# Dilated attention of one block: dense scores against all keys, or two sparse parts over a residue order

## The reference, cut to what matters

```python
DILATED_PATTERNS = ((128, 1), (512, 4), (2048, 16))
def dilated_window_attention(q, k, v, rel_bias, dilation, half_steps):
    """Each query attends to positions i + j*dilation, |j| <= half_steps.
    Returns normalised output (B,H,S,dh) f32 and log-sum-exp (B,H,S) f32."""
    ...
def mixer_dilated(q, k, v, rel_bias):
    outs, lses = [], []
    for window, dilation in DILATED_PATTERNS:
        o, lse = dilated_window_attention(q, k, v, rel_bias, dilation, window // (2 * dilation))
        ...
    w = jax.nn.softmax(jnp.stack(lses, 0), axis=0)
    return jnp.einsum('pbhs,pbhsd->bhsd', w, jnp.stack(outs, 0))
```

## Time and profile before

| what | value |
|---|---|
| median of three executions | 4218.14 us |
| the profiled execution, by the same clock | 4229.26 us |
| its span | 4227.5 us |
| PE, DVE, ACT, POOL busy, share of the span | 90%, 50%, 47%, 29% |
| attention stage, dilated heads (first to last unit) | 187.4 us of the span |
| attention stage, latent heads (first to last unit) | 218.0 us of the span |

### The profile page before, as it was taken

One profiled execution on the slowest core, in us unless ns is written; L12 is line 12 of the kernel. 1 busy time (PEld: TensorE's weight loads), 2 busy tenths in 40 slices (PEclk: granted clock), 3 DMA queues, 4 the chain that ended last, 5 costly groups with the idle time before them and its releaser, 6 DMA issues. The chain is left out here.

```text
span 4227.5 us, 55120 instructions
## 1 busy us (share of the span) xinstructions
PE 3820.9 (90%) x20567; PEld 3209.4 (76%) x20567; DVE 2119.5 (50%) x3777; ACT 1981.5 (47%) x3487; POOL 1233.9 (29%) x732
## 2 busy tenths in 40 slices
PE   8989997969986999999488875797999999999998
PEld 6879996847755777887388875797888768888886
DVE  3348875267754333320566757674234237533453
ACT  5248766337756545522366654564324234323331
POOL 0024430000004322311133244121631103876541
PEclk9999998969998999999699997998999999999999
DMA  3744223479957222222322212113653112222542
GB/s 118 251 134 118 51 51 105 184 273 420 421 241 255 90 80 80 89 94 74 90 61 79 80 55 79 46 46 115 227 161 117 68 50 90 87 88 85 188 148 98
DMA packets 336536, 548.38 MB, mean 130 GB/s; under 512 B 116451, under 2 KB 209507, under 8 KB 325219
## 3 DMA queue, kind: packets, MB, share of 16 engines
q1 hardware_dynamic: 318348, 478.76, 34.1%
q10 hardware_dynamic: 10720, 39.85, 2.4%
q0 software_dynamic: 7200, 26.22, 1.6%
HBM read 400.63 MB, written 144.11 MB: 129 GB/s over the span
## 5 line engine op out<-in xcount | busy, mean ns | idle before, releaser
L2739 POOL TENSOR_TENSOR mid_w_lo<-mid_w_raw,mid_w_hi 128x1024 fp32r<-128x1024 f32 (+1 forms) x64 | 153.0, 2395 | 406.2 <-ACT mid_w_hi L2927 406.2
L3473 POOL TENSOR_TENSOR end_w_lo<-end_w_raw,end_w_hi 128x1024 fp32r<-128x1024 f32 x60 | 147.2, 2460 | 334.4 <-ACT end_w_hi L3815 334.3
L3097 PE MATMUL mid_ps<-mid_w_hi,mid_xT_hi 128*128 128x512 f32 x576 | 229.0, 398 | 2.7 <-DVE mid_xT_lo L2801 2.7
L3097 PE MATMUL mid_ps<-mid_w_lo,mid_xT_hi 128*128 128x512 f32 x576 | 224.7, 390 | 0.0
L3097 PE MATMUL mid_ps<-mid_w_hi,mid_xT_lo 128*128 128x512 f32 x576 | 224.7, 390 | 0.0
L4131 PE MATMUL end_ps<-end_w_hi,end_xT_hi 128*128 128x512 f32 x544 | 214.7, 395 | 0.0
L4131 PE MATMUL end_ps<-end_w_hi,end_xT_lo 128*128 128x512 f32 x544 | 212.3, 390 | 0.0
L4131 PE MATMUL end_ps<-end_w_lo,end_xT_hi 128*128 128x512 f32 x544 | 211.9, 390 | 0.0
L957 DVE SCALAR_TENSOR_TENSOR moe_w_lo<-moe_wgu,moe_gcol,moe_w_hi 128x512 fp32r<-128x512 f32 x272 | 185.5, 746 | 7.7 <-ACT moe_w_hi L1097 7.7
L343 ACT ACTIVATE att_pT_hi<-att_pT_ps 128x512 fp32r<-128x512 f32 x256 | 139.1, 596 | 99.7 <-PE att_pT_ps L36 99.6
L1097 ACT ACTIVATE moe_w_hi<-moe_wgu,moe_gcol 128x512 fp32r<-128x512 f32 x272 | 173.2, 715 | 2.5 <-DMA moe_wgu<-in_w_gate_up 2.5
(11 more groups left out here) (641 smaller groups left out, 11565.8 us busy)
## 6 DMA issues: line engine op xcount, KB each, us to landing
moe_wgu<-in_w_gate_up SPq DMA_DIRECT2D x34, 2048.0 KB, 11.6
moe_wd<-in_w_down SPq DMA_DIRECT2D x34, 1024.0 KB, 14.1
mid_w_raw<-in_w_in SPq DMA_DIRECT2D x60, 512.0 KB, 4.0
end_w_raw<-in_w_ffn_out SPq DMA_DIRECT2D x44, 512.0 KB, 3.7
end_w_raw<-in_w_ffn_in SPq DMA_DIRECT2D x40, 512.0 KB, 4.3
expert_rows<-moe_out ACTq DMA_DIRECT2D x34, 512.0 KB, 11.3
in_tail<-mid_y SPq DMA_DIRECT2D x56, 256.0 KB, 2.1
qkvT<-mid_conv SPq DMA_DIRECT2D x24, 512.0 KB, 4.4
```

The source lines that it names most:

```text
L2739: pool.tensor_tensor(w_lo[:, c % 2, 2 * q:2 * q + 2, 0:wid], w_raw[:, 2 * q:2 * q + 2, 0:wid], w_hi[:, c % 2, 2 * q:2 * q + 2, 0:wid].bitc ...
L3097: ins = pe.matmul(o_, lhsT, rhs, start=(k == 0 and part == 0), stop=(k == KC - 1 and part == 2))
L3473: pool.tensor_tensor(halves(w_lo, piece), w_raw[:, 2 * q:2 * q + 2], halves(w_hi, piece).bitcast(F32), ALU.subtract).then_inc(w_split, 1)
```

## The change

The tokens are put in residue order when x is loaded: first all tokens that are 0 modulo 4, then 1, 2 and 3; outputs are stored back in token order, in four transfers each. A new function `attend_both` replaces `attend_heads` for this stage (the second layer keeps `attend_heads`). It alternates one dilated head (four units) and one latent head (eight units), so a pair of heads has 12 units and the stage 96.

A dilated unit covers 256 queries with four segments of 256 scores: two "near" segments (128 queries of all four classes against 64 keys of each class, from reordered queries `q_near`) and two "far" segments (128 queries of one class against the 256 keys of this class). Each segment has its own maximum, exponential, sum and product with values; for the product the turned weights are the stationary operand, sixteen matmuls of 128 columns. ScalarE copies the low half of each outcome out of PSUM and VectorE adds the high half into `keep`. When a dilated head's four units are through, its near outcomes with their maxima and sums (66 floats a row) are stored to DRAM and loaded again in the order of the far ones (`move_near`); VectorE and ScalarE find the weights of the two parts (`highest`, `share`), and GpSimd merges them (`merge`). Latent units are computed as before. The bias rows shrink from 2048 to 1184 floats a head (three banks), and a dilated head's table comes in ten transfers, its values in seven.

```diff
+STRIDE = 4
+NEAR, AFAR = 96, 512
+BIAS = (2 * STRIDE - 1) * NEAR + AFAR
...
+def attend_both(nc, name, ident_dram, dilated, latent):
+    SPARSE_UNITS, SEGS, SEG = 4, 4, 2 * P
+    jobs = [job for pair in zip(dilated, latent) for job in pair]
...
+                def load_table(j):
...
+                    for w in range(2):
+                        sp.dma_start(view[:, w + 1, 0], first).then_inc(table_in[i % 2], 16)
+                        sp.dma_start(view[:, w, 1], second).then_inc(table_in[i % 2], 16)
+                    sp.dma_start(view[:, 0, 0, :, EDGE:], first[:, :, EDGE:]).then_inc(table_in[i % 2], 16)
+                    sp.dma_start(view[:, 2, 1, :, 0:EDGE], second[:, :, 0:EDGE]).then_inc(table_in[i % 2], 16)
+                    for c in range(STRIDE):
+                        sp.dma_start(table[c * BLOCK:(c + 1) * BLOCK, i % 2, 3 * SEG:], far[c]).then_inc(table_in[i % 2], 16)
...
+                def move_near(j):
+                    i = rank[j]
+                    sp.wait_ge(kept, sparse_by[last_unit[j]])
+                    for c in range(STRIDE):
+                        dst = jobs[j]["near"][c * CLASS:(c + 1) * CLASS].rearrange("(t u) d -> u t d", u=BLOCK)
+                        sp.dma_start(dst, keep[c * BLOCK:(c + 1) * BLOCK, i % 2, 0]).then_inc(near_out, 16)
+                    sp.wait_ge(near_out, 16 * STRIDE * (i + 1))
+                    sp.dma_start(keep[:, i % 2, 2], jobs[j]["near"].rearrange("(t p) d -> p t d", p=P)).then_inc(near_in, 16)
+
+                def store(j):
+                    if sparse[j]:
+                        sp.wait_ge(merged, rank[j] + 1)
+                    else:
+                        sp.wait_ge(o_out, rank[j] + 1)
+                    for c in range(STRIDE):
+                        src = o[:, j % 2, c * NT // STRIDE:(c + 1) * NT // STRIDE]
+                        sp.dma_start(jobs[j]["out"][c], src).then_inc(o_stored[j % 2], 16)
+
+                for i in range(H // 2 + 1):
+                    if i < H // 2:
+                        load(2 * i)
+                        load(2 * i + 1)
+                    if i:
+                        move_near(2 * i - 2)
+                        store(2 * i - 2)
+                        store(2 * i - 1)
...
+                def weigh_sparse(n):
...
+                    for g in range(SEGS):
+                        i = 2 * t + g % 2
+                        for b in range(2):
+                            v = near_both[:, rank[j] % 2, i + b] if g < 2 else v_both[:, j % 2, 2 * t + b]
+                            for k, part in enumerate((pT_hi, pT_lo)):
+                                ins = pe.matmul(oT_ps[:, g * P:(g + 1) * P], split_at(part, n)[:, 2 * g + b], v,
+                                                start=(b == 0 and k == 0), stop=(b == 1 and k == 1))
...
+                    if n >= 5 and is_sparse[n - 5]:
+                        act.wait_ge(weighed, weighed_by[n - 5])
+                        act.activation(low[:, n % 2], oT_ps[:].rearrange("p (g d) -> p g d", d=P)[:, :, DV:], ACT.Copy).then_inc(low_set, 1)
...
+                    for g in range(SEGS):
...
+                        ch.add(dve.tensor_tensor_reduce(biased[:, n % 2, here], s_ps[:, n % 2, here], table[:, i, at:at + SEG],
+                                                        1.0, -3e38, ALU.add, ALU.max, keep[:, i, g // 2, w, DV:DV + 1]))
...
+                def highest(j):
+                    both = keep[:, rank[j] % 2, 1:3]
+                    dve.wait_ge(near_in, 16 * (rank[j] + 1))
...
+                for n in range(U + 6):
+                    for j in range(0, H, 2):
+                        if n == last_unit[j] + 7:
+                            highest(j)
+                    if n >= 5 and n - 5 < U and is_sparse[n - 5]:
...
+                        dve.wait_ge(low_set, sparse_by[n - 5])
+                        dve.tensor_tensor(keep[:, rank[j] % 2, 0:2, 2 * t:2 * t + 2, 0:DV], found, lows, ALU.add).then_inc(kept, 1)
...
+                        if not sparse[j] and n == last_unit[j] + 6:
...
+                            dve.tensor_tensor(o[:, j % 2], o_ps[:], inverse[:, i % 2].unsqueeze(2).to_broadcast([P, NT, DV]), ALU.mult).then_inc(o_out, 1)
...
+                for j in range(H):
+                    if j:
+                        split_queries(j)
+                    if sparse[j]:
+                        order_queries(j)
+                    if j:
+                        split_keys(j)
+                    split_values(j)
...
+                    if sparse[j] and j:
+                        merge(j - 2)
...
-                for b in range(4):
-                    pe.matmul(ps[0:A_HEADS, 4 + b], values[:], onehot[:, b * BANK:(b + 1) * BANK], start=True, stop=True).then_inc(hot_done, 1)
+                for b in range(BIAS_BANKS):
+                    wid = min(BANK, BIAS - b * BANK)
+                    pe.matmul(ps[0:A_HEADS, 4 + b, 0:wid], values[:], onehot[:, b * BANK:b * BANK + wid], start=True, stop=True).then_inc(hot_done, 1)
...
-    attend_heads(nc, "att", ident, dilated + latent)
+    attend_both(nc, "att", ident, dilated, latent)
```

More of the change, by code:

```diff
@@ new lines, in bias_constants, with reach @@
+def bias_constants(T, buckets, max_distance, patterns):
+    block, edge = P // STRIDE, P // STRIDE // 2
+    steps = np.arange(NEAR)[None] - (block + edge - 1)
+    near = (STRIDE * steps + np.arange(1 - STRIDE, STRIDE)[:, None]).reshape(-1)
+    far = STRIDE * (np.arange(AFAR) - (T // STRIDE - 1))
+    def reach(rel, pairs):
+        n = np.abs(rel)
+        return sum(((n % d == 0) & (n // d <= w // (2 * d)) & (n < T)).astype(np.float64) for w, d in pairs)
+    assert all(d == 1 or d % STRIDE == 0 for w, d in patterns)
+    rel = np.concatenate([near, far])
+    count = np.concatenate([reach(near, [(w, d) for w, d in patterns if d == 1]), reach(far, [(w, d) for w, d in patterns if d > 1])])
@@ L467, in dilation_constants, with by_class @@
     onehot = (np.arange(buckets)[:, None] == bucket[None]).astype(np.float32)
-    count = sum(((n % d == 0) & (n // d <= w // (2 * d)) & (n < T)).astype(np.float64) for w, d in patterns)
     log_count = np.where(count > 0, np.log(np.maximum(count, 1)), -1e30)
     return np.concatenate([onehot, log_count[None].astype(np.float32)], 0)
+def by_class(rows):
+    return np.ascontiguousarray(rows.reshape(-1, STRIDE, rows.shape[1]).transpose(1, 0, 2).reshape(rows.shape))
 def rotary_tables(T, theta, half):
@@ L2155, in table_step @@
                         sp.wait_ge(rows_in, 16 * (h + 1))
-                        sp.dma_start(skew[h].rearrange("(p w) -> p w", w=W), raw[:, 0:W]).then_inc(rows_out, 16)
+                        for c in range(STRIDE):
+                            rows = P // STRIDE
+                            at = c * (rows * BIAS + NEAR - rows)
+                            dst = skew[h, at:at + rows * BIAS].rearrange("(p w) -> p w", w=BIAS)
+                            sp.dma_start(dst, raw[c * rows:(c + 1) * rows, 0:BIAS]).then_inc(rows_out, 16)
                     else:
@@ L4210, in table @@
-    def table(h):
-        return skew[h:h + 1, P - 1:P - 1 + P * W - P].rearrange("h (p w) -> (h p) w", w=W - 1)[:, 0:W - P]
-    dilated = [dict(depth=A_DIM, dv=A_DIM, q=qkT_a[h * A_DIM:(h + 1) * A_DIM], k=qkT_a[AW + h * A_DIM:AW + (h + 1) * A_DIM],
-                    v=tiles(v_a[:, h * A_DIM:(h + 1) * A_DIM]), out=tiles(mixed[:, h * A_DIM:(h + 1) * A_DIM]),
-                    scale=A_DIM ** -0.5, bias=table(h)) for h in range(A_HEADS)]
-    latent = [dict(depth=NOPE + ROPE, dv=B_DIM, q=qkT_b[h], k=qkT_b[B_HEADS + h],
-                   v=tiles(v_b[:, h * B_DIM:(h + 1) * B_DIM]),
-                   out=tiles(mixed[:, AW + h * B_DIM:AW + (h + 1) * B_DIM]), scale=(NOPE + ROPE) ** -0.5, bias=None) for h in range(B_HEADS)]
@@ L4219, in build_program, with tables, block, far @@
-    attend_heads(nc, "att", ident, dilated + latent)
+    mixed, near = dram("mixed", (T, AW + B_HEADS * B_DIM)), dram("near", (A_HEADS, T, A_DIM + 2))
+    def tables(h):
+        rows, width, pitch = P // STRIDE, BIAS - 1, STRIDE * NEAR
+        def block(ahead):
+            at = (STRIDE - 1) * NEAR + rows - 1 + ahead
+            flat = skew[h, at:at + P * width].rearrange("(p w) -> p w", w=width)
+            return flat[:, 0:pitch].rearrange("p (c z) -> p c z", z=NEAR)[:, :, 0:rows]
+        def far(c):
+            at = c * (rows * width + NEAR - rows) + (2 * STRIDE - 1) * NEAR + P - 1
+            return skew[h, at:at + rows * width].rearrange("(p w) -> p w", w=width)[:, 0:3 * P]
+        return block(0), block(rows), [far(c) for c in range(STRIDE)]
@@ new lines, in by_class_out @@
+    def by_class_out(columns):
+        return mixed[:, columns].rearrange("(h p c) d -> c p h d", c=STRIDE, p=P)
+    dilated = [dict(depth=A_DIM, dv=A_DIM, q=qkT_a[h * A_DIM:(h + 1) * A_DIM], k=qkT_a[AW + h * A_DIM:AW + (h + 1) * A_DIM],
```

(4 more changed lines are left out.)

446 lines of the change are left out of this document (428 added, 18 removed).

## The result

The changed kernel took 4265.69 us (median of four executions, 4254.07 to 4266.53), the kernel before 4219.65 us beside it: ratio 1.0101, 95% interval 1.0082 to 1.012. It is 46 us slower; the forecast was 4220.5 us, with 4180 to 4256 as its range. The profiled execution took 4265.32 us, its span is 4263.2 us, 35.7 us more than the profiled span of before.

The account below looks back on a forecast made before the run. PE's own issue was taken to bound the stage before the change. Stage +1.9, later start +2.2, last store +1.3 and front -3.0 sum to +2.4 us on 4218.1: 4220.5 us, range 4180 to 4256.

Parts of the forecast that it names:

- The circle: SP's list and VectorE's wait for the near part feed each other: A + B = 53.5 us a pair, six pairs.
- A: From the normalising through SP's loads and the near part's trip to its landing: 23.3 us, bounds 18.0 and 27.
- first pair: Start of the stage up to the first normalising, with no move behind loads: 63.5 us.
- last pair: Six steps remaining behind the last circle: 22.8 us.
- B: VectorE's steps from the near part's arrival to the next normalising: 30.2 us, ends 27 and 31.5.
- the three latent loads: Latent queries, keys and values ahead of the near stores: issued from 12.7 us, 4.2 us of transfers, ending about 18.1.
- rival 4: SP's queue stalls in issuing the small table and value pieces, A = 27: +22 us, 4242.5 us, chance 0.17.
- The fall of the clock: PE stands about 6 us in VectorE's wait, then one step runs at the lower clock: 1.7 us added in B.
- rivals 2 and 3: Sparse weighing: 2, bound by moving columns, 0.06 us, 4208.5 us, chance 0.05; 3, float32 price, 0.222 us, 4245 us, chance 0.12.
- rival 1: The near part's move is nearly hidden: A = 18.0, B = 28.0, 46.0 us a pair, 4175.5 us, chance 0.14.
- The front: Before the stage, the one-hot product shrinks from 2048 to 1184 columns: -3.0 us, bounds -3.0 and 0.
- The tail: The stage's last store becomes four issues: 1.3 us more.

Follow-up runs that it names:

- e7_start: Changed kernel with the first latent head's queries and keys loaded before the first table and values, and split before the first queries are ordered: span 4263.6 us.
- best2: Changed kernel with merge three units later, latent loads behind the near part's trip, first latent head early: 4197.57 us, ratio 0.9933 to the kernel before.
- e1_no_trip: Changed kernel without the near part's four stores, load and VectorE's wait for them (merge takes rows that don't belong together): span 4193.2 us.

## Why the prediction missed, step by step

The circle held as a mechanism. One of its halves, A, was sized too short, and a wait of the first pair was put at nothing. The stage came out 29.8 us longer than forecast (449.1 us where 417.3 + 1.9 was forecast), and by the parts of the sum: six circles 21.2, first pair 10.8, last pair -2.2. (The sum began at 275.60 us; counted from the first score at 273.45 its first pair is 63.5 + 2.2 = 65.7 us.)

**The trip, A (27.3 for 23.3): the step that failed most.** Four terms, means over the circles. First near store 16.7 us after the normalising's end against 14.3: the table's pieces took 6.8 us, not 5.0, as one or two of the short-run pieces held the queue for 1.3 to 2.2 us, and the values 3.8, not 3.3. The four near stores 2.5 us to issue, not 1.5. From there to the load 4.5, as forecast (4.3). Landing 2.9, not 3.2. Another 0.7 is the normalising itself: A begins at its start in the table, at its end in the prediction, which counts it in B. By the prediction's bounds A is 26.6 for 23.3 and B 30.5 for 30.2. One step of the sum had no row: the three latent loads, issued from 12.7 us on with 4.2 us of transfers, end by these figures at 16.9 and not at 18.1; the 4.5 us measured from the last near store to the load leave the end as it was. I took the middle, "since the unloaded issues are the commoner rows"; but a list whose engines are 0.86 busy is not unloaded, and the upper bound, 27, was nearly the value. That was rival 4, with 4242.5 us; the rest of the miss lies elsewhere. I had held eight small stores without a stall against it, which ran with the DMA engines 0.24 busy (2148.7 to 2152.7 us). The Trainium skill's price for small transfers ("DMA: Bandwidth & Descriptors", section "Bandwidth", measured there on transfers that GpSimd issues) would, by an estimate, have made that rival's surplus about twice as large; A at 27.3 does not agree with that.

**The first pair (76.5 us from the first score to the first normalising, forecast 65.7).** I gave it no wait. But GpSimd's list has the first values ahead, for which it waits 3.4 us, and then splits the latent queries and keys one after another; PE waited 5.0 us for the keys. Its clock had fallen to the lower level at about 281 us, ahead of that wait, when PE had stood 2.2 us for VectorE, and came back only at 301 us. GpSimd's split of the keys, and PE's last transposes ahead of the wait and first latent score, in order of time:

```profile
285.33 2.34 POOL L926 TENSOR_TENSOR att_k_lo<-att_kT,att_k_hi 96x1024 fp32r<-96x1024 f32 x1
```

```profile
280.81 1.94 PE L40 MATMUL att_pT_ps<-att_ident,att_p 128*128 128x128 f32 x8 [2.16 <-DVE att_pT_lo L878]
287.77 0.76 PE L677 MATMUL att_s<-att_k_hi,att_q_hi 96*128 96x512 f32 x1 [5.02 <-issue]
```

e7_start and best2 took 6.1 and 12.8 us off the first normalising by changing that order; from the first score to it they take 66.1 and 64.6 us, with the clock at its upper level from 277.9 and 273.8 us on, so without this wait the forecast's 65.7 holds. The prediction read GpSimd's passes for the later pairs and not for the first.

**B (29.8 for 30.2): right in sum, in part by luck.** The fall of the clock was forecast at 1.7 us; an early and a late return differ by about 1 us, and no run isolates what the fall costs in whole. The units themselves were dearer than forecast, which e1_no_trip shows without any wait: its pairs took 45.6 us against 43.3, of which 1.9 in the four sparse steps (3.15, 4.36, 4.37 and 3.20 us, means over the circles, for 4 x 3.3) and 0.4 in the first latent one. In each of the first three of these VectorE's `neg_top` stands behind a GpSimd pass (0.4 to 0.6, 0.6 and 1.7 us in place of 0.17). I had priced it by an estimate of 0.1 us. How much of the 1.9 us these operations make up, no run isolates.

**What held.** Weighing matmuls of 128 columns start 0.11 us apart, the row that I chose over both bounds, so rivals 2 and 3 fall; the 81 ns of the Trainium skill ("TensorE: Matmul & The Clock Gate", "Back-to-back issue gap") do not agree with this float32r stream. PE in order of time:

```profile
310.04 0.28 PE L711 MATMUL att_oT_ps<-att_v_both,att_pT_lo 128*128 128x128 f32 x1
310.15 0.27 PE L711 MATMUL att_oT_ps<-att_v_both,att_pT_hi 128*128 128x128 f32 x1
310.26 0.28 PE L711 MATMUL att_oT_ps<-att_v_both,att_pT_lo 128*128 128x128 f32 x1
```

Latent steps with sparse weighing take 4.1 us (the first, with its fold, 4.9), those without 3.2 to 3.6, free sparse steps 2.9 to 3.2. VectorE's wait comes in the six circles and hardly in the first and last pair (0.7 and 0.1 us), as forecast, but it is 11.2 to 12.5 us long and not 7 to 9. So rival 1, the nearly hidden move, falls.

**Around it.** The front gave more than the 3.0 us forecast: its one-hot product takes 4.1 instead of 7.0 us, as forecast, and starts 0.8 us earlier, the attention's first load is issued 4.8 us earlier (257.80 against 262.61; two executions of the kernel before differ by 1.5 us there), and 2.0 of that are lost again before the first score to the ordering of the queries and its loads, near the 2.2 forecast. The tail cost 0.7 instead of 1.3.

**The base.** Carrying 11 us over from the profiled execution to the median was wrong: the kernel before runs from 4217.86 to 4230.10 us, and three executions at its low end made a base 6.7 us under the middle of the others (4224.8 us, nine executions beside best2). With stage and base right, the remaining 6 us between the traces lie in untouched stages; what causes them stays open.

## What to carry to other kernels

A round trip through DRAM in the one queue that also prefetches is as long as everything ahead of it in the list, in issues and in bytes; put it ahead of what is needed latest, and its consumer so late in the list that other work covers it. When a wait closes a circle with the list that feeds it, find its length by summing both halves, and take the prices of issues from a stretch in which the DMA engines are as busy as they will be there. Read the first round of a pipeline on its own: its loads and splits have no round before to hide in.

## What the runs showed of the hardware that was not expected

A small VectorE operation can take ten times its time beside GpSimd: `neg_top` of 128 x 4 took 0.17 us alone and up to 1.72 us beside a pass of GpSimd, ending 0.02 to 0.03 us behind it, while the form of 128 x 1 took 0.14 to 0.16 us in all 128 cases. The Trainium skill, "SBUF — State Buffer", section "SBUF: two separate sides", has VectorE's two-port modes and GpSimd exclude each other for a whole instruction, the later one blocked. These rows agree with that; which mode an instruction ran in, no trace shows.

The clock came back from its lower level 2.9 to 3.1 us after PE had started again in two circles and 5.3 to 5.8 us in four, behind idle times of PE of much the same length (9.4 and 10.0 us, and 9.9 to 10.7); a step of 3.1 us became one of 4.0 to 4.2. And a second issuing queue didn't shorten a load of 264 KB but lengthened it, from 2.9 to 5.9 us, as it met the other queue's loads (DMA engines 0.94 busy instead of 0.45).
